# Normed input and arena 128 bytes from the weights' parts, modulo 512, in place of 192

## What is computed

```python
for l in range(2):                                   # first block
    mod = silu(c) @ ada_w[l] + ada_b[l]              # shifts, scales, gates
    h = h + 0.5 * g1 * swiglu(modulate(rms_norm(h)), ffn1_w_in[l], ffn1_w_out[l])   # D_FF = 2816
    z = modulate(rms_norm(h)) @ w_in[l]              # attention, conv, gating, forgetting attention
    h = h + g2 * (mixed @ w_out[l])
    h = h + 0.5 * g3 * swiglu(modulate(rms_norm(h)), ffn2_w_in[l], ffn2_w_out[l])
for l in range(2):                                   # second block
    proj = rmsnorm(x) @ w_in_2[l]                    # q, k, v of 24 heads, three gates
    x = x + (gates * branches) @ w_o_2[l]
    x = x + square(relu(rmsnorm(x) @ w_up_2[l])) @ w_down_2[l]
return rmsnorm(x)
```

## Time and profile before

| | us |
|---|---|
| Median of 3 runs | 2025.19 |
| Lowest and highest of them | 2023.29, 2029.39 |
| The profiled execution, its time | 2022.61 |
| Its span, first to last instruction | 2020.8 |
| TensorE busy in the span | 1944.2 |
| Mean granted TensorE clock | 0.982 of 2.4 GHz |

### The profile page before, as it was taken

How to read it: one execution, slowest core, us unless ns; L and a number is a source line. 1 busy time by engine, 2 the same in 40 slices (tenths; PEclk the granted TensorE clock), 3 DMA queues, 4 the chain that set the end, 5 groups by cost and what they waited for, 6 DMA issues and landing times.

```text
span 2020.8 us, 36133 instructions
## 1 busy us (share of the span) xinstructions
PE 1944.2 (96%) x15216; PEld 1870.4 (93%) x15216; DVE 835.4 (41%) x1747; ACT 940.4 (47%) x1467; POOL 1320.6 (65%) x612
## 2 busy tenths in 40 slices
PE   7999997999999999889999999999999999999999
PEld 3999996899999999779999999989999999989999
DVE  3774577382147466745112622233311622233322
ACT  2544454344454445444444445525543445525543
POOL 0888760388878887316887964506897964505896
PEclk8999998999999999899999999999999999999999
DMA  9999650695589885217545643336664643335662
GB/s 321 359 345 308 198 185 22 207 365 181 185 302 365 279 264 187 84 63 267 192 161 173 209 157 110 125 118 189 200 204 152 209 148 112 124 121 188 199 201 99
DMA packets 357075, 398.01 MB, mean 197 GB/s; under 512 B 9017, under 2 KB 319025, under 8 KB 356913
## 3 DMA queue, kind: packets, MB, share of 16 engines
q1 hardware_dynamic: 356752, 395.50, 59.0%
q10 hardware_dynamic: 160, 0.20, 0.0%
HBM read 394.62 MB, written 1.05 MB: 196 GB/s over the span
## 4 chain that ended last, share of the span: by engine, by line
PE 85%; DVE 4%; SPq 3%; ACT 3%; POOL 2%; DMA 1%; issue 1%; ACTq 0%; DVEq 0%
PE bank L716 67%; PE bank L800 6%; PE bank L1124 3%; POOL w_lo L682 2%; PE bank L929 1%; PE bank L963 1%; SPq L577 1%; SPq L544 1%; DVE bank L1653 1%; PE bank L747 1%; ACT w_hi L1204 1%; DVE arena L1724 1%; PE bank L751 1%; PE bank L1025 1%; SPq L587 1%
## 5 line engine op out<-in xcount | busy, mean ns | idle before, releaser
L682 POOL TENSOR_TENSOR w_lo<-ring,w_hi 128x1024 fp32r<-128x1024 f32 (+2 forms) x608 | 1320.4, 2197 | 685.3 <-ACT w_hi L1204 684.7
L716 PE MATMUL bank<-hn,w_hi 128*128 128x256 f32 x2752 | 773.5, 281 | 5.9 <-POOL w_lo L682 5.0
L1204 ACT ACTIVATE w_hi<-ring 128x1024 fp32r<-128x1024 f32 (+2 forms) x608 | 578.5, 976 | 409.9 <-PE bank L716 368.2
L716 PE MATMUL bank<-hn_lo,w_hi 128*128 128x256 f32 x2752 | 764.8, 278 | 0.0
L716 PE MATMUL bank<-hn,w_lo 128*128 128x256 f32 x2752 | 764.7, 278 | 0.0
L716 PEld LDWEIGHTS bank<-hn,w_hi 128*128 128x128 f32 x2752 | 519.5, 189 | 10.1 <-POOL w_lo L682 6.0
L716 PEld LDWEIGHTS bank<-hn_lo,w_hi 128*128 128x128 f32 x2752 | 518.5, 188 | 1.2 <-issue 0.5
L716 PEld LDWEIGHTS bank<-hn,w_lo 128*128 128x128 f32 x2752 | 518.0, 188 | 0.0
L716 PE MATMUL bank<-gated,w_hi 128*128 128x256 f32 x1408 | 248.9, 281 | 0.0
L716 PEld LDWEIGHTS bank<-gated,w_hi 128*128 128x128 f32 x1408 | 217.0, 190 | 0.0
L716 PE MATMUL bank<-gated,w_lo 128*128 128x256 f32 x704 | 197.8, 281 | 0.0
(11 more groups left out here) (209 smaller groups left out, 2226.1 us busy)
## 6 DMA issues: line engine op xcount, KB each, us to landing
ring<-in_ffn_w_in SPq DMA_DIRECT2D x88, 1024.0 KB, 7.5
ring<-in_w_in SPq DMA_DIRECT2D x72, 1024.0 KB, 5.1
arena<-in_ada_w SPq DMA_DIRECT2D x35, 2048.0 KB, 10.5
ring<-in_w_up SPq DMA_DIRECT2D x32, 1024.0 KB, 5.4
ring<-in_w_down SPq DMA_DIRECT2D x32, 1024.0 KB, 5.1
ring<-in_ffn_w_out SPq DMA_DIRECT2D x32, 768.0 KB, 5.1
ring<-in_ffn_w_out SPq DMA_DIRECT2D x32, 640.0 KB, 4.1
ring<-in_w_in SPq DMA_DIRECT2D x16, 512.0 KB, 3.6
```

What stands on the lines that cost most here:

```text
L682: pool.tensor_tensor(w_lo[:, q, ks], ring[:, r, k0:k0 + n], w_hi[:, q, ks], ALU.subtract) \
L716: last = mm(out, a, b, start=start and i == 0, stop=stop and i == 2)
L1204: f(w_hi[:, q, half * 4:half * 4 + n], ring[:, r, k0:k0 + n], ACT.Copy).then_inc(weights_rounded, 1)
```

## The change

The filler ahead of `hn` shrinks from 48 to 32 words, 192 to 128 bytes. Everything allocated behind it begins 64 bytes lower: `hn`, `hn_lo`, the squares, the constants, the small tables and the arena. `ring`, `w_hi`, `w_lo` and `h` stay.

```diff
--- before.py
+++ after.py
@@ -398,7 +398,7 @@
         ring = sb("ring", RING, 8, 256)
         w_hi, w_lo = sb("w_hi", 2, 8, 256, dtype=F32R), sb("w_lo", 2, 8, 256, dtype=F32R)
         h = sb("h", KT, S)
-        hn_start = sb("hn_start", 48)
+        hn_start = sb("hn_start", 32)
         hn, hn_lo = sb("hn", KT, S, dtype=F32R), sb("hn_lo", KT, S, dtype=F32R)
         square, square_sum = sb("square", 2, S), sb("square_sum", S)
         rstd = sb("rstd", S)
```

## The result

The changed kernel takes 2068.6 us (median of 4 runs, 2064.1 to 2073.8) against 2025.4 us before: the ratio is 1.0212, with a 95% interval of 1.0197 to 1.0227. It is slower by 43 us; 2025 was forecast, and the range ended at 2058. The profiled execution has a span of 2067.1 us against 2020.8 before.

The account below looks back on a forecast made before the run. The prediction took line 716's split matmuls on TensorE, count times interval, as the bound. It added 0 for interval lengths, rhythm share and other engines to 2022.6 us, predicting 2025 us against the median, range 2000 to 2058.

Parts of the forecast that it names:

- What bounds the kernel: Whole kernel: TensorE busy 96% of 2020.8 us; time is the number of line 716's split matmuls times the interval between them.
- Two rhythms, drawn at interruptions: Line 716's streams: steady intervals of 113.4 or 117.9 ns per matmul, one of them drawn whenever the stream is interrupted.
- No cost outside TensorE: Other engines and DMA: same patterns 64 bytes lower, costed at nothing; uncovered part at a norm's hand-over 0.2 us.
- Two distances, 192 and 320, give the same pair: Line 716: offsets of moving operand from weights' parts only place their meeting within a matmul; effect on interval lengths 0.
- The bound above: Line 716, if lengths move: one more step of 4.4 ns on 12768 matmuls, 56 us on top, about 2081 us.
- The case: Line 716: the interval itself gets longer, up to about 2081 us; chance 0.05.
- The slower rival: Restarts behind norms and attention: short-rhythm streams fall into the long one, 20 to 33 us, 2045 to 2058; chance 0.29.
- a length that moved: Line 716: interval itself changes either way, about 1973 to 2081 us; chance 0.05 up, 0.04 down.
- The share of the rhythms: Line 716: about 5250 matmuls long, 7500 short; change taken as 0, ends +33 us all long, -23 us all short.
- The faster rival's trend: Pieces behind line 837 and the 912: long streams turn short, later meeting favouring it; 2009 or down to 2002; chance 0.25.
- The 109.2 ns: Line 716: skill page's back-to-back interval for 256 columns; reaching it would save 76 us, giving 1949 us.

## Why the prediction was wrong

- **What bounds the kernel** was right: line 716, its matmuls times their interval. 39.6 of the 46.3 us are in its eleven long pieces.
- **Two rhythms, drawn at interruptions** was right for distance 192: nine kernels with distances of that kind show the same two numbers, and small matmuls ahead of a stream redraw them. The one with the weights' parts 128 bytes apart comes near the long one on its token-major products alone.
- **No cost outside TensorE** was right. With everything moved by 448 bytes and the distance kept, the ratio is 0.9986.
- **The step that failed** is "Two distances, 192 and 320, give the same pair. I take it that 128 does too: effect on the two lengths 0." The measured effect at 128 is 5.4 to 6.7 ns on a matmul of the short rhythm and 0.9 to 2.2 ns on one of the long. The two samples were no independent ones: they are the same modulo 128, the period with which the good places come. The model behind it, that both operands run evenly and meet once per matmul wherever they start, has no place for such a period; with it, 256 would be as good as 192, and it has 120.0 ns against 113.3. Its premise stood in no row either: in the earlier trace rows a load takes 0.19 us, longer than the 0.11 to 0.12 us from one matmul to the next, and nothing there says how its reads lie in that time. What the operands do to each other inside the matmul stays open; what is shown is that their distance sets the interval.
- **The bound above** (one more step of 4.4 ns, 2081 us) held for the time, but not as a bound for one matmul, which can lose 6.7 ns. The case had a chance of 0.05. It was the one that came, and since 128 was in no row, a length that no row shows deserved far more.
- **Slower than the range.** The slower rival gave at most 2058 us by 117.8 ns on all. Its mechanism, a draw of the rhythm, is not what happened: its mark, 175.3 us for 1488 matmuls, is not there (178.57), and the mark of a length that moved, a third number in the divisions, is.
- **The share of the rhythms** was taken at 0. At 128 the pair is another, 118.7 and 120.0 ns, and lies 1.3 ns apart in place of 4.4, so that a draw weighs less there. At the good distances the share moved the time between kernels from 0.9905 (the kernel without the long rhythm on `hn`, `gated` and `up`) to 1.0074 of before, 34 us where 56 lie between the bounds. The prediction's counts of 7500 short and 5250 long should be 7416 and 5352 by its own rule of half and half, which moves the bounds by under 1 us.
- **The faster rival's trend** (the later the meeting, the better) falls: 128 lies later than 192 and is worse.
- **The rules that it weighed.** The 109.2 ns were reached by no stream; the shortest has 113.3. The Trainium skill's rule in "SBUF — State Buffer", section "Who interferes with whom", that TensorE's read ports for the moving operand and for the weights are independent and that it never waits for anyone, would have made all these kernels equal. The measurements decide against it as a full account: the slowest and the fastest lie 74 us apart (2079.3 and 2005.7), and they do the same work with only the places of buffers changed.

## What to carry to other kernels

Where TensorE is the chain, divide the chain's long pieces by their matmuls before anything else: two numbers for the same work mean that an address or a phase is in play. Where the stationary and the moving operand of fp32r matmuls begin, modulo 256, is then a tuning knob, worth 3.7% from the best to the worst kernel found here (single runs), and a filler of a few words sets it; try all steps of it rather than infer one from two others, since samples can share a period that they don't show. The plain fp32 matmuls of this kernel did not respond to it. A result of one such filler holds for the buffers it moves together: each product had its own distance.

## What the runs showed of the hardware that was not expected

- A stream of 128 x 128 by 256 fp32r matmuls, at a granted clock of 1.00 (2.4 GHz), starts one every 113.3 or 117.8 ns with moving and stationary operand 64 bytes apart modulo 128, one every 120.0 ns with both alike modulo 256, and every 117.3 to 120.0 ns at the four other distances tried (128, 160, 208, 224, and 384 like 128); 16 bytes off a good place give 119.2 ns.
- 256 bytes more change nothing: 128 and 384 agree to the nanosecond, and 0 and 256 both give 120.0 ns.
- At 128 bytes there are two rhythms as well, 118.7 and 120.0 ns, and at 160 there are 117.3 and 118.7.
- Plain fp32 matmuls of the same shape (line 1124: 256 of them in 55.7 us) take the same time in the kernels before and after and with the arena at 256.
- With the two weights' parts 128 bytes apart modulo 256, the 117.8 ns rhythm was in no long stream on `hn`, `gated` or `up` in two profiled executions of one kernel; with 0, or 256, it was. Whether the spacing forbids it, and why, is open, as is which load the moving operand has to keep away from.
- None of this stands in waits: the stall is inside the matmul, 276 ns in the best case and 285 ns in the worst group without waits (`up` with `w_lo` at 128), and TensorE counts as busy throughout.
